# The prelude of a transformer layer: modulation vectors and sums of squares moved from VectorE sums to one-column TensorE products

## The reference, cut to what matters

```python
mod = jax.nn.silu(c) @ w_ada[l] + b_ada[l]
shift1, scale1, gate1, shift2, scale2, gate2 = [m[:, None, :] for m in jnp.split(mod, N_MOD, axis=-1)]

h = rms_norm(x, norm_attn[l]) * (1.0 + scale1) + shift1      # rms_norm: x * rsqrt(mean(x*x) + EPS) * g
proj = h @ w_in[l]
...
x = x + gate1 * (mixed @ w_out[l])
h = rms_norm(x, norm_ffn[l]) * (1.0 + scale2) + shift2
ffn = (jax.nn.silu(h @ w_gate[l]) * (h @ w_up[l])) @ w_down[l]
x = x + gate2 * ffn
```

## Time and profile before

| what | value |
|---|---|
| time, median of 3 runs | 1500.77 us (1498.84 to 1502.93) |
| the profiled execution | 1499.38 us, its span 1497.6 us |
| TensorE busy | 1393.3 us, 93% of the span |
| VectorE busy | 658.2 us, 44% |
| ScalarE busy | 476.2 us, 32% |
| GpSimd busy | 86.3 us, 6% |
| first `proj_tile` product (L1288) | at 78.3 us |

### The profile page before, as it was taken

One profiled execution on the slowest core, in us unless ns is written; L12 is line 12 of the kernel. 1 busy time (PEld: TensorE's weight loads), 2 busy tenths in 40 slices (PEclk: granted clock), 3 DMA queues, 4 the chain that ended last, 5 costly groups with the idle time before them and its releaser, 6 DMA issues.

```text
span 1497.6 us, 18059 instructions
## 1 busy us (share of the span) xinstructions
PE 1393.3 (93%) x6960; PEld 1165.0 (78%) x6960; DVE 658.2 (44%) x921; ACT 476.2 (32%) x727; POOL 86.3 (6%) x84
## 2 busy tenths in 40 slices
PE   2899999787999989969989999999999999999998
PEld 1788878776887778768868888888888888887886
DVE  8633444676557888864372111111111112334333
ACT  3512212455336666842132111111111112222221
POOL 1600100221000000010000000000000000001001
PEclk9799999998999999969999999999999999999999
DMA  9052432000001000300131111111111113224322
GB/s 382 25 216 98 168 126 88 1 1 1 1 1 43 1 1 1 141 1 29 56 140 57 42 56 42 56 42 42 56 42 56 42 56 127 97 90 175 128 98 98
DMA packets 24995, 109.56 MB, mean 73 GB/s; under 512 B 2800, under 2 KB 2928, under 8 KB 23408
## 3 DMA queue, kind: packets, MB, share of 16 engines
q1 hardware_dynamic: 22608, 100.47, 18.6%
q0 software_dynamic: 2336, 8.39, 1.5%
HBM read 100.46 MB, written 8.39 MB: 73 GB/s over the span
## 4 chain that ended last, share of the span: by engine, by line
PE 77%; DVE 14%; issue 4%; POOL 2%; ACT 2%; DVEq 0%; DMA 0%; SPq 0%; POOLq 0%; ACTq 0%
PE ps L1288 45%; PE ps L1277 8%; PE ps L1279 8%; PE ps L1278 8%; DVE left L1083 4%; PE ps L1484 2%; PE ps L1506 1%; DVE acc L846 1%; PE ps L1493 1%; DVE beta L1087 1%; PE ps L1473 1%; POOL rstd L408 1%; PE ps L1564 1%; DVE sqs L831 1%; POOL rstd L410 1%
## 5 line engine op out<-in xcount | busy, mean ns | idle before, releaser
L825 DVE TENSOR_TENSOR WL<-raw,WH 128x1024 fp32r<-128x1024 f32 x114 | 141.1, 1238 | 457.3 <-ACT WH L462 457.3
L462 ACT ACTIVATE WH<-raw 128x1024 fp32r<-128x1024 f32 x114 | 120.3, 1056 | 357.7 <-PE ps L1288 185.1
L1288 PE MATMUL ps<-h2H,WH 128*128 128x512 f32 x672 | 207.0, 389 | 0.0
L1288 PE MATMUL ps<-h2L,WH 128*128 128x512 f32 x672 | 206.9, 389 | 0.0
L1288 PE MATMUL ps<-h2H,WL 128*128 128x512 f32 x672 | 206.8, 389 | 0.0
L1288 PEld LDWEIGHTS ps<-h2H,WH 128*128 128x128 f32 x672 | 126.0, 188 | 26.4 <-DVE WL L825 0.2
L1288 PEld LDWEIGHTS ps<-h2L,WH 128*128 128x128 f32 x672 | 126.1, 188 | 26.2
L1288 PEld LDWEIGHTS ps<-h2H,WL 128*128 128x128 f32 x672 | 126.1, 188 | 26.2
L1277 PE MATMUL ps<-TH,WH 128*128 128x512 f32 x352 | 137.1, 389 | 1.0 <-DVE yst L1249 1.0
L1278 PE MATMUL ps<-TL,WH 128*128 128x512 f32 x352 | 137.0, 389 | 0.0
L1279 PE MATMUL ps<-TH,WL 128*128 128x512 f32 x352 | 136.9, 389 | 0.0
(11 more groups left out here) (243 smaller groups left out, 2180.1 us busy)
## 6 DMA issues: line engine op xcount, KB each, us to landing
ada<-ada SPq DMA_DIRECT2D x12, 2048.0 KB, 8.0
raw<-gu SPq DMA_DIRECT2D x44, 512.0 KB, 3.4
raw<-down SPq DMA_DIRECT2D x44, 512.0 KB, 3.5
raw<-win SPq DMA_DIRECT2D x18, 512.0 KB, 3.2
x_in<-xT SPq DMA_DIRECT2D x4, 1024.0 KB, 8.3
raw<-wout SPq DMA_DIRECT2D x8, 512.0 KB, 4.0
x<-xT SPq DMA_DIRECT2D x1, 4096.0 KB, 12.9
x_spill_d<-x SPq DMA_DIRECT2D x1, 4096.0 KB, 12.6
```

Source lines behind the costliest of these rows:

```text
L462: A(WH[par % 2][:], raw[r % 2][:], ACT.Copy).then_inc(sem["split_h"], 1)
L825: V.tensor_tensor(WL[par % 2][:], raw[r % 2][:], WH[par % 2][:], ALU.subtract).then_inc(sem["split_l"], 1)
L1288: last = mm(ps[:, b + hf, :], l[s][:, j * P:(j + 1) * P], r[:, j, 512 * hf:512 * hf + 512], start=(j == 0 and k == 0), stop=(j == KD - 1 a ...
```

## The change

Four edits, all in the prelude.

1. Sums of squares. `sqs`, the 7 additions, the transposes and the VectorE sum are gone. TensorE takes each `sq[j]` as it comes: for each of the 8 token tiles, one float32 product with 128 columns of `sq` as weights and one column of ones as the moving operand, added up in 8 columns of PSUM bank 5: 64 products. ScalarE's square `j` waits for the products of square `j - 2`.
2. Statistics. The mean is one VectorE operation on 8 columns of PSUM; `wsplit(0, 0)` follows it and `wsplit(1, 1)` comes after the diagonals, which are now two operations of 4 tiles each. The broadcast's two halves wait for one of them each.
3. Modulation. `acc1` and VectorE's sums are gone. `adaln1(g)` on TensorE is now 32 float32 one-column products (4 columns by 8 `k`) in place of 8.
4. `h`. ScalarE writes `hH` straight from the normalized token chunk (Identity with scale and bias, rounded to fp32r), then `h` in place by the same operation. VectorE makes `hL = h - hH`; GpSimd's 8 subtractions are gone. VectorE normalizes two chunks ahead.

```diff
 # GpSimd
-        for j in range(KD):
-            pool.wait_ge(sem["hH_done"], j + 1)
-            nc.gpsimd.tensor_tensor(hL[:, j, :], x_in[:, j, :], hH[:, j, :], ALU.subtract).then_inc(sem["hL_done"], 1)
 # ScalarE
-            if j >= 3:
-                act.wait_ge(sem["x_add"], j - 2)
-            A(sq[j % 2][:] if j else sqs[:], x_in[:, j, :], ACT.Square).then_inc(sem["x_sq"], 1)
+            if j >= 2:
+                act.wait_ge(sem["x_mm"], j - 1)
+            A(sq[j % 2][:], x_in[:, j, :], ACT.Square).then_inc(sem["x_sq"], 1)
...
+            A(hH[:, j, :], x_in[:, j, :], ACT.Identity, scale=a1[:, j:j + 1], bias=mod1[:, j:j + 1]).then_inc(sem["hH_done"], 1)
             A(x_in[:, j, :], x_in[:, j, :], ACT.Identity, scale=a1[:, j:j + 1], bias=mod1[:, j:j + 1]).then_inc(sem["h_done"], 1)
-            act.wait_ge(sem["h_done"], j + 1)
-            A(hH[:, j, :], x_in[:, j, :], ACT.Copy).then_inc(sem["hH_done"], 1)
 # VectorE
-        for j in range(1, KD):
-            dve.wait_ge(sem["x_sq"], j + 1)
-            if j >= 2:
-                dve.wait_ge(sem["x_add"], j - 1)
-            V.tensor_tensor(sqs[:], sqs[:], sq[j % 2][:], ALU.add).then_inc(sem["x_add"], 1)
-        def adaln1(g, between=None):
...
+        dve.wait_ge(sem["x_mm"], KD)
+        V.tensor_scalar(ms[:, 0, :], ps[:, 5, 0:NT], 1.0 / D, EPS, ALU.mult, ALU.add).then_inc(sem["stat_ms"], 1)
         wsplit(0, 0)
+        dve.wait_ge(sem["stat_r"], 1)
+        for hf in range(2):
+            t = slice(4 * hf, 4 * hf + 4)
+            V.tensor_tensor(diag1[:, t, :], ident[:].unsqueeze(1).broadcast_to([P, 4, P]), rms[:, 0, t].unsqueeze(2).broadcast_to([P, 4, P]), ALU.mult).then_inc(sem["stat_diag"], 1)
         wsplit(1, 1)
...
+        dve.wait_ge(sem["stat_bc"], 2)
+        normalize(0)
+        normalize(1)
         for g in range(KD // 2):
+            scale_shift(g)
             for j in (2 * g, 2 * g + 1):
+                if j + 2 < KD:
+                    normalize(j + 2)
+                h_low(j)
 # TensorE
-        pe.wait_ge(sem["x_add"], KD - 1)
-        for tt in range(NT):
-            last = nc.tensor.transpose(ps[:, 4 + tt // 4, tt % 4 * P:(tt % 4 + 1) * P], sqs[:, tt * P:(tt + 1) * P], ident[:])
-        last.then_inc(sem["x_turned"], 1)
+        for j in range(KD):
+            pe.wait_ge(sem["x_sq"], j + 1)
+            for tt in range(NT):
+                last = mm(ps[:, 5, tt:tt + 1], sq[j % 2][:, tt * P:(tt + 1) * P], ones[:, 0:1], start=(j == 0 and tt == 0), stop=(j == KD - 1), skip_group_check=True)
+            last.then_inc(sem["x_mm"], 1)
...
-            pe.wait_ge(sem["acc1_done"], g + 1)
             for m in range(4):
                 w = slice(m * P, (m + 1) * P)
-                mm(ps[:, 4 + g % 2, m:m + 1], ada1[:, g, KD - 1, w], silu_c[:, KD - 1:KD], start=True, stop=False, skip_group_check=True)
-                last = mm(ps[:, 4 + g % 2, m:m + 1], acc1[g % 2][:, w], ones[:, 0:1], start=False, stop=True, skip_group_check=True)
+                for k in range(KD):
+                    last = mm(ps[:, 4 + g % 2, m:m + 1], ada1[:, g, k, w], silu_c[:, k:k + 1], start=(k == 0), stop=(k == KD - 1), skip_group_check=True)
```

## The result

The changed kernel takes 1540.83 us (median of 4 runs, 1535.86 to 1541.06) against 1499.8 (4 runs, 1498.44 to 1502.93): a ratio of 1.0263, 95% interval 1.0247 to 1.0279. It is slower by 41 us, where +41.4 and 1541 were forecast. The profiled execution took 1541.06, its span is 1539.3.

The account below looks back on a forecast made before the run. TensorE was taken to bound the changed prelude from 8.4 us on, but for 2.8 us of statistics; `proj_tile` would begin at 119.7 instead of 78.3, +41.4 us on the profiled 1499.38, so 1541 us, range 1531 to 1548.

Parts of the forecast that it names:

- Step 1: Sums of squares on TensorE: 64 one-column products at 0.427 us, 27.3 us, from 8.4 to 35.7.
- Step 2: Statistics and broadcast: mean at 35.8, TensorE starts at 38.5, two broadcasts take about 3.5 us, free at 42.0.
- Step 3: Modulation on TensorE: four groups of 32 one-column products at 0.427 us, 54.7 us; groups 0 and 1 before the first chunk.
- Step 4: The chunks on TensorE: 96 products of 512 columns, 0.427 us each at 1.2 GHz, 0.227 at 2.4; no waits for `hL`.
- the rises: TensorE's clock going to 2.4 GHz for about 3.4 us, saving 3.1 each; together 6.7 us before group 3 ends.
- the last 66 products: Chunk products after modulation group 3: 4.4 us at the lower clock, then 12.6 at the upper, 17.0 us in all.
- The hidden parts: Prelude work on VectorE, ScalarE and loads that never sets the end: 9.8 us of low parts, 1.4 us more ScalarE.
- A: Prelude on TensorE: one-column products count as activity and raise the clock; +1.3 us, 1501, no change; 4 in 100.
- B: Prelude on TensorE: one-column products hold a raised clock but don't raise it; +14 us, 1515; 5 in 100.
- C: Prelude on TensorE: long one-column runs pack tighter at a raised clock, 0.194 us or less each; faster, 1495; 1 in 100.

Follow-up runs that it names:

- the filler: The changed kernel with an unused 512-column bfloat16 identity product behind each one-column product of the sums of squares, but the last: 1552.47 us, ratio 1.0362.
- the clock raised beforehand: The changed kernel with 6 unused 512-column float32 products of ones put on TensorE ahead of the sums of squares: 1539.54 us, ratio 1.0260.
- split roles: The kernel before, with sums of squares on TensorE by 512 moving columns, VectorE's modulation sums begun earlier, low parts on GpSimd: 1507.59 us, ratio 1.0049.

## Why the prediction was right

**The bound and the mechanism.** Right: 128 and 256 one-column rows, most of them at 1.2 GHz, on a chain that TensorE holds. Undoing the parts gave back 27.5 and 13.1 us; swapping the operands of both gave back 32 us, with the same time for TensorE at one clock. The Trainium skill's rule in the form weighed above ("TensorE: Matmul & The Clock Gate", Part 1) does not hold for one-column products: TensorE worked without a gap from 43.95 to 71.0 at 0.21 us a row.

**Step 1.** Forecast 8.4 to 35.7; measured 9.07 to 36.5, so 27.45 us for 27.3. The start is 0.7 later, since the first `x_in` landed later in this execution (first square at 7.87, at 7.33 before).

**Step 2.** Forecast 2.7 us to the broadcast, measured 3.6. The mis-sized term is GpSimd's power: 2.52 us against 1.69. The prediction laid `wsplit(0, 0)` inside it at no cost. The changed kernel, then the kernel before:

```profile
36.63 1.22 DVE L818 TENSOR_TENSOR WL<-raw,WH 128x1024 fp32r<-128x1024 f32 x1
36.86 2.51 POOL L382 TENSOR_TENSOR rms<-ms,nhalf 128x8 f32<-128x8 f32 x1 [33.84 <-DVE ms L821]
```

```profile
23.55 1.68 POOL L384 TENSOR_TENSOR rms<-ms,nhalf 128x8 f32<-128x8 f32 x1 [20.52 <-DVE ms L856]
```

The subtraction had begun first and kept its 1.22 us; the power grew by 0.83, about the time that the two overlap. All 13 kernels agree: in the 7 with the subtraction there the power took 2.51 to 2.53 us, in the 6 where VectorE was idle 1.67 to 1.69. None of them moves `wsplit` alone.

**Step 3.** Groups 0 and 1: 27.1 us for 27.3, no rise. Group 2 took 10.45 and group 3 9.58 of 13.66, both begun at the upper clock.

**Step 4 and the rises.** Savings of 6.7 us were forecast ahead of the last 66 products. Measured: 3.2 in group 2, 2.0 in chunks 2 and 3 (5.7 us for 7.7), 4.1 in group 3: 9.3 in all. None followed the broadcasts. In other kernels one did: groups 0 and 1, begun behind the same two broadcasts, took 24.0 us with the squares back on VectorE and 24.1 with the filler, but 27.1 with the clock raised beforehand. So the broadcasts alone don't settle whether a rise follows them. The last stretch took 17.3 for 17.0. So about 2 us of lateness and 2.6 of extra rises cancel: 119.2 for 119.7. Agreement to 0.5 us is partly luck: one rise more or less is 3.1 us, and the range was drawn for that. One of the four runs took 1535.86, 5 us less than the others; more rises could do that, but no trace of it shows its cause.

**The hidden parts.** Low parts, the second ScalarE operation and the loads behind the first `x_in` never came into the chain. VectorE waited 36.4 us for TensorE's groups.

**The rivals.** A: refuted by 0.21 us a row through 27 us of unbroken work. B: refuted by the raised clock that fell at 12.9. Its 1515 counts from the median; from the profiled execution, as the forecast does, it would be 1513. C: long runs do pack a little tighter, 0.21 us a product at 2.4 GHz (32 rows in 3.35 us from 76.05) where eight in a row had 0.223, but that is still over the 0.194 that C needed, and most ran at 1.2.

## What to carry to other kernels

Before work is moved to an idle TensorE, price it at the clock that this very work leaves, not at the peak: a matrix times a vector with the matrix as weights moves one column, and here the squares took 27.45 us that way and 15.4 with the matrix moving. If a reduction goes there, let the large operand move, keep TensorE's dense work together, and leave VectorE a share sized by rows. Look also at what GpSimd's work costs its neighbour: subtractions that take VectorE 9.8 us itself held it up for 4.5 us on GpSimd in one order and 10.2 in another.

## What the runs showed of the hardware that was not expected

- GpSimd's subtraction of two SBUF operands (2.43 us) stretches VectorE's SBUF sums beside it: three rows 4.29 us against 2.33, one of 0.48 to 2.56. VectorE's normalizations, which read one tile from SBUF and one from PSUM, were not stretched: two took 2.35 us (from 59.01 in the kernel before) with a subtraction beside them from 59.37. Without GpSimd's subtractions the 24 sums of the modulation take 18.0 us, with them 22.0 (old order) or 24.0 (split roles).
- GpSimd's power of 128 x 8 took 2.51 to 2.53 us beside a VectorE subtraction begun before it (7 kernels) and 1.67 to 1.69 without (6).
- A 512-column bfloat16 identity product between one-column products left the clock at 1.2 GHz, and hid about 0.19 us of the next product's loads.
- Before the first recorded rise PEclk reads 1.00 though TensorE runs at 1.2 GHz (64 rows in 13.4 us up to 71.0 in the changed kernel); the spacing of the rows tells the level.
